# First two products of a transformer kernel interleaved by depth block, their transfers in that order, and the last product finished bank by bank

## What is computed

```python
def _even_mixer(x, norm_g, w_in, ...):
    h = _rmsnorm(x, norm_g)
    qa, ka, va, qb, kb, vb = _split(h @ w_in, EVEN_SPLITS)   # 512, 128, 128, 512, 512, 512 columns
    qa = _rmsnorm(qa per head, qn_a)
    ...
def rmsnorm(x, g):
    y = xf * lax.rsqrt(jnp.mean(xf * xf, axis=-1, keepdims=True) + RMS_EPS)
    return (y * g).astype(x.dtype)
# last: x = x + merged @ w_out; out = rmsnorm(x, g_final)
```

## Time and profile before

| | |
|---|---|
| median of the runs | 973.5 us |
| the profiled execution | 973.11 us |
| its span | 971.3 us |
| PE, share of the span | 99% |
| VectorE | 73% |
| ACT | 57% |
| POOL | 16% |

### The profile page before, as it was taken

One profiled execution on the slowest core, in us unless ns is written; L12 is line 12 of the kernel. 1 busy time (PEld: TensorE's weight loads), 2 busy tenths in 40 slices (PEclk: granted clock), 3 DMA queues, 4 the chain that ended last, 5 costly groups with the idle time before them and its releaser, 6 DMA issues.

```text
span 971.3 us, 13894 instructions
## 1 busy us (share of the span) xinstructions
PE 963.1 (99%) x5288; PEld 825.0 (85%) x5288; DVE 705.0 (73%) x1093; ACT 555.1 (57%) x957; POOL 154.9 (16%) x189
## 2 busy tenths in 40 slices
PE   9999999999999999999999999999999999999997
PEld 8878888888888888888888888888888888988885
DVE  6888676776666767786667656666758989888884
ACT  6688665444555553455456444554535857866662
POOL 2741018920001102220001000000550110000000
PEclk9999999999999999999999999999999999999999
DMA  9885535565554664445555665555544453543631
GB/s 338 302 226 190 181 130 181 188 229 183 173 194 155 216 215 131 131 135 212 174 174 181 203 211 185 173 186 183 206 153 152 154 194 111 173 153 129 217 131 44
DMA packets 110338, 174.72 MB, mean 180 GB/s; under 512 B 4288, under 2 KB 73024, under 8 KB 110272
## 3 DMA queue, kind: packets, MB, share of 16 engines
q1 hardware_dynamic: 109840, 173.40, 53.3%
q10 hardware_dynamic: 432, 0.44, 0.1%
HBM read 172.78 MB, written 1.05 MB: 179 GB/s over the span
## 4 chain that ended last, share of the span: by engine, by line
PE 92%; DVE 3%; POOL 1%; issue 1%; DMA 1%; SPq 1%; ACT 0%; POOLq 0%; DVEq 0%
PE ps L572 24%; PE ps L542 14%; PE ps L500 9%; PE ps L445 8%; PE ps L447 8%; PE ps L446 8%; PE ps L546 7%; PE ps L509 5%; PE ps L521 2%; PE ps L700 1%; PE ps L680 1%; PE ps L530 1%; PE ps L668 1%; DMA xs<-in_x 1%; PE ps L624 1%
## 5 line engine op out<-in xcount | busy, mean ns | idle before, releaser
L1557 DVE TENSOR_TENSOR wlo<-raw,whi 128x1024 fp32r<-128x1024 f32 x312 | 373.9, 1237 | 13.7 <-PE ps L572 8.3
L1047 ACT ACTIVATE whi<-raw 128x1024 fp32r<-128x1024 f32 x312 | 315.8, 1049 | 35.0 <-PE ps L572 22.0
L572 PE MATMUL ps<-whi,ur 128*128 128x512 f32 x656 | 182.0, 390 | 0.0
L572 PEld LDWEIGHTS ps<-whi,ur 128*128 128x128 f32 x656 | 121.1, 188 | 23.5
L542 PE MATMUL ps<-hT,whi 128*128 128x512 f32 x592 | 140.5, 389 | 0.0
L542 PEld LDWEIGHTS ps<-hT,whi 128*128 128x128 f32 x592 | 110.7, 188 | 22.8
L445 PE MATMUL ps<-whi,hT 128*128 128x512 f32 (+1 forms) x312 | 122.1, 391 | 0.0
L447 PE MATMUL ps<-whi,hT 128*128 128x512 f32 (+1 forms) x312 | 120.0, 385 | 0.0
L446 PE MATMUL ps<-wlo,hT 128*128 128x512 f32 (+1 forms) x312 | 119.9, 384 | 0.0
L1924 DVE TENSOR_TENSOR arena<-ps,arena 128x256 f32<-128x256 f32 x80 | 33.4, 423 | 98.6 <-ACT arena L1289 98.6
L1289 ACT ACTIVATE arena<-ps 128x256 f32<-128x256 f32 x80 | 30.2, 385 | 127.2 <-PE ps L546 127.2
(11 more groups left out here) (232 smaller groups left out, 1284.4 us busy)
## 6 DMA issues: line engine op xcount, KB each, us to landing
raw<-in_w SPq DMA_DIRECT2D x64, 1024.0 KB, 5.6
raw<-in_w_in SPq DMA_DIRECT2D x34, 1024.0 KB, 4.9
raw<-in_w_in_o SPq DMA_DIRECT2D x24, 1024.0 KB, 5.2
raw<-in_w_out_o SPq DMA_DIRECT2D x8, 1024.0 KB, 4.8
raw<-in_w_in_e SPq DMA_DIRECT2D x5, 1024.0 KB, 13.2
raw<-in_w_mem SPq DMA_DIRECT2D x4, 1024.0 KB, 11.1
raw<-in_w_out_e SPq DMA_DIRECT2D x4, 1024.0 KB, 4.9
raw<-in_w_out SPq DMA_DIRECT2D x4, 1024.0 KB, 4.8
```

The source lines that it names most:

```text
L572: mm = e.matmul(bank("acc", stage, 2 * tb + i), x[p], t[p % 2][:, 0, 512 * i:512 * i + 512], start=start and p == 0, stop=stop and p == 2)
L1047: e.activation(split_half(i)[0], raw_half(i), ACT.Copy).then_inc(*up("hi", ("hi", i)))
L1557: e.tensor_tensor(l, raw_half(i), h.bitcast(F32), ALU.subtract).then_inc(*up("lo", ("lo", i)))
```

## The change

The first two products, qa and ka, take turns: two depth blocks of qa, then the same two depth blocks of ka (for both position blocks), four times. Within qa a pass now runs over both position blocks before the next pass. The transfers come in that order: x block 0 first, on SP's queue, then the weights, with the ka tile in four transfers of 256 KB and the x blocks 0 to 3 one by one. ACT and VectorE make the parts in that order; the high part of x block 0 is VectorE's. There are eight warm-up products for ten. What ACT and VectorE do behind these first weights keeps its order. At the end the last four depth blocks run bank by bank, the final norm is made for each bank, and the last scale is split at column 640 for 512 between VectorE and ACT.

```diff
@@ sp_program
+                first_block(0)
+                piece(0, 0, 1, "w0")
+                piece(0, 1, 1, "w1")
+                first_block(1)
+                piece(2, 0, 2, "w6")
+                piece(0, 2, 1, "w2")
+                first_block(2)
+                piece(0, 3, 1, "w3")
+                first_block(3)
+                piece(2, 2, 2, "w8")
+                piece(1, 0, 1, "w4")
+                first_pair(2)
+                piece(1, 1, 1, "w5")
+                piece(2, 4, 2, "w9")
+                first_pair(3)
+                piece(1, 2, 2, "raw1")
+                piece(2, 6, 2, "raw2")
...
-            for tb, i in ((0, 1), (0, 0), (1, 0)):
+            for tb, i in ((0, 0), (0, 1), (1, 0)):
+                n = (slice(0, 640), slice(640, 1024))[i]
...
@@ pe_program
+            def first_products():
+                qa, ka = ([take("mm", label, tb) for tb in range(2)] for label in ("qa", "ka"))
+                for j in range(4):
+                    i = first_half["qa"] + j
...
+                    for k in (2 * j, 2 * j + 1):
...
+                        for tb in range(2):
+                            e.matmul(qa[tb], xh[tb], h[:, k % 2, :], start=k == 0, stop=False)
+                        w.wait_ge(*at("lo" if k % 2 else "lo0", i))
+                        for tb in range(2):
+                            e.matmul(qa[tb], xh[tb], l[:, k % 2, :], start=False, stop=False)
+                        w.wait_ge(*at("xl", "E", k))
+                        for tb in range(2):
+                            mm = e.matmul(qa[tb], xl[tb], h[:, k % 2, :], start=False, stop=k == 7)
...
+                    i = first_half["ka"] + j // 2
...
+                    for tb in range(2):
+                        for k in (2 * j, 2 * j + 1):
...
+                            mm = mm3(ka[tb][:, 0:256], x, (h[:, k % 4, :], l[:, k % 4, :]), k == 0, k == 7)
...
-            for i in range(10):
+            for i in range(8):
                 e.matmul(psum[7][:, 0:128], arena[:, 0:128], arena[:, 128:256], start=True, stop=True)
-            qa_product()
-            for j in range(2):
-                n_half("ka", j, 256, "E")
...
+            first_products()
...
             for tb in range(2):
-                for d in range(4):
-                    acc_part("sec", ur[0], d, t[d], tb, by_bank if d == 3 else by_pass, False, d == 3)
+                for c in range(2):
+                    for d in range(4):
+                        acc_part("sec", ur[0], d, t[d], tb, [(p, c) for p in range(3)], False, d == 3)
@@ act_program
+            def weights_first():
+                for j in range(4):
+                    for k in range(2):
+                        w.wait_ge(*((S[f"w{2 * j + k}"], 16) if j < 3 else loaded(1)))
+                        e.activation(split_half(j)[0][:, k, :], raw_half(j)[:, k, :], ACT.Copy).then_inc(
+                            *up("hi", ("hi", j) if k else ("hi0", j)))
+                        if j or k:
+                            x_first(2 * j + k)
+                    i, t = 4 + j // 2, slice(2 * (j % 2), 2 * (j % 2) + 2)
...
+                    e.activation(split_half(i)[0][:, t, :], raw_half(i)[:, t, :], ACT.Copy).then_inc(
...
-            e.dma_start(xT0[:, 0, :], A["xT"][0:128, :]).then_inc(S["t0"], 16)
-            weights_to(6)
+            weights_first()
             row_squares("E", x3, osb, [(S["x0"], 16), (S["x1"], 16)])
             hn_squares("qa")
             used("qa", 3)
...
@@ dve_program
-            weights_to(6)
+            e.tensor_scalar(hT[0][:, 0, :], xT0[:, 0, :], gain[:, G_ATT:G_ATT + 1], None, ALU.mult).then_inc(*up("dev", ("xh", "E", 0)))
+            weights_first()
             row_reciprocals("E")
             hn_sums("qa")
...
                 for i in range(2):
+                    n = slice(512 * i, 512 * i + 512)
+                    acc_added("sec", banks=(2 * tb + i,))
                     w.wait_ge(*at("x", "sec", 2 * tb + i))
...
+                    e.tensor_tensor(fin[:, tb, n], x3[:, tb, n], rows[:, R_FIN + 512 * i:R_FIN + 512 * i + 512], ALU.mult).then_inc(
+                        *up("dst", ("xg", tb, i)))
+                    w.wait_ge(*at("sq", "fin", tb, i))
...
-                e.scalar_tensor_tensor(fin[:, tb, 0:512], x3[:, tb, 0:512], s1, rows[:, R_FIN:R_FIN + 512],
-                                       ALU.mult, ALU.mult).then_inc(*up("dst", ("fin", tb, 0)))
+                e.tensor_scalar(fin[:, tb, 0:640], fin[:, tb, 0:640], s1, None, ALU.mult).then_inc(*up("dst", ("fin", tb, 0)))
```

More of the change, by code:

```diff
@@ L35 @@
 SEMS = ["mm", "wd", "tp", "qk", "pv", "hi", "xh", "aev", "ex", "asq", "lo", "xl", "dev", "dst", "sc", "po",
-        "w0", "w1", "w2", "w3", "w4", "w5", "w6", "w7", "raw0", "raw1", "raw2", "raw3", "x0", "x1", "t0", "t1", "t2", "t3", "t4", "id", "c", "c2", "g", "b", "m", "out"]
+        "w0", "w1", "w2", "w3", "w4", "w5", "w6", "w7", "w8", "w9", "raw0", "raw1", "raw2", "raw3", "x0", "x1", "t0", "t1", "t2", "t3", "t4", "t5", "id", "c", "c2", "g", "b", "m", "out"]
 PAIRS = [(0, 2), (1, 3), (4, 6), (5, 7)]
@@ L377, in sp_program @@
                 if m == 0:
[L378 to L392, removed]
+                    first_weights()
+                elif m < 3:
+                    pass
                 elif m == 3:
@@ L1034, in weights_to @@
                 for i in range(done[0], min(n, NH)):
[L1035 to L1041, removed]
                     if tiles[i // 2][0] == "memT":
                         continue
-                    w.wait_ge(*((S[f"w{i // 2 + 4}"], 16) if i in (4, 6) else loaded(i // 2)))
+                    w.wait_ge(*((S["w7"], 16) if i == 6 else loaded(i // 2)))
                     if i >= NHI:
@@ L1048, in weights_to @@
                 done[0] = max(done[0], n)
+            def weights_first():
[7 more added lines that the diff above has]
+                    i, t = 4 + j // 2, slice(2 * (j % 2), 2 * (j % 2) + 2)
+                    w.wait_ge(*((S[("w6", "w8", "w9")[j]], 16) if j < 3 else loaded(2)))
+                    e.activation(split_half(i)[0][:, t, :], raw_half(i)[:, t, :], ACT.Copy).then_inc(
+                        *up("hi", ("hi", i) if j % 2 else ("hi0", i)))
+                done[0] = 6
             def used(label, j):
@@ L1544, in weights_to @@
                     h, l = split_half(i)
[L1545 to L1551, removed]
                     if tiles[i // 2][0] == "memT":
@@ L1558, in weights_to, with weights_first @@
                 done[0] = max(done[0], n)
+            def weights_first():
+                for j in range(4):
+                    h, l = split_half(j)
+                    for k in range(2):
+                        w.wait_ge(*(at("hi", j) if k else at("hi0", j)))
+                        e.tensor_tensor(l[:, k, :], raw_half(j)[:, k, :], h[:, k, :].bitcast(F32), ALU.subtract).then_inc(
+                            *up("lo", ("lo", j) if k else ("lo0", j)))
+                        x_first(2 * j + k)
+                    i, t = 4 + j // 2, slice(2 * (j % 2), 2 * (j % 2) + 2)
+                    h, l = split_half(i)
+                    w.wait_ge(*(at("hi", i) if j % 2 else at("hi0", i)))
+                    if i >= NLO:
+                        w.wait_ge(*at("wd", i - NLO))
+                    e.tensor_tensor(l[:, t, :], raw_half(i)[:, t, :], h[:, t, :].bitcast(F32), ALU.subtract).then_inc(
+                        *up("lo", ("lo", i) if j % 2 else ("lo0", i)))
+                done[0] = 6
             def memory_low(blocks):
```

69 lines of the change are left out of this document (37 added, 32 removed).

## The result

The changed kernel takes 975.09 us (median of 15 runs, 974.46 to 976.47) beside 973.05 for the kernel before (15 runs). That is 2.0 us more by the medians; the ratio of the runs is 1.0025, 95% interval 1.0018 to 1.0032. The forecast was 974.7 in 973.2 to 976.0, so the time lies in the range and on the side that was named. Between "within", which had 0.83, and "slower", which had 0.15, it lies on the edge: the text's bound in us, 975.45, is not reached, while its 0.2% is just passed, by a ratio whose interval holds 1.002. The profiled execution is one of the lower group, 974.83 us with a span of 973.0.

A forecast was written before the change was run, and what follows sets the result against it. TensorE, busy 99% of the span, was taken to bound the kernel, so any new hole is paid in full. Lateness before qb of +1.4 and tail of -0.2 gave +1.2 on 973.5: 974.7 us, range 973.2 to 976.0.

The forecast's parts named there:

- within: Whole kernel: a time within about 0.2%, 1.95 us, of no change; chance 0.83.
- slower: Whole kernel: a time above 975.45 us; chance 0.15.
- The mechanism: Before qb: qa ends later, ACT's fixed order holds half 6 behind qa's squares, PE stands for about 1.85 us.
- rival 4: Front: small transfers land late, ACT waits for raw1 past 15.4; 975.7 or 976.3 for landings at 16.4 or 17; chance 0.15.
- The lateness: Start of qb: 1.5 us late by the sum, 24.05 for 22.56; taken as 1.4, span 1.2 to 2.0.
- The term for the first pair: First qa and ka blocks on PE: holes of 0.3 and 0.1 us waiting for low parts, 0.4 in all.
- It passed in full: From qb to the end: VectorE's chain is fed by PE, so the 0.9 us wait at kb's transposes swallows nothing; +1.4.
- Rival 2: At kb's transposes, 64.5 us: VectorE's chain less late than PE, so 0.9 us is swallowed; 973.8; chance 0.13.
- Rival 1: Front: PE's start 0.65 us earlier carries through to qb, not slower; 972.7; chance 0.10.
- Rival 3: POOL's first scale of qa's sums shut out by VectorE's low parts, 1.5 us later; 974.9; chance 0.07.
- The clock: TensorE in the new hole before qb: no fall of the granted clock expected, as it was still full in 967 to 968.
- The tail: After the last product: 0.1 each from the moved small step and the shorter last scale, 0.2 us saved (0 to 0.3).

The follow-up runs named there:

- lower group: Nine of the changed kernel's 15 runs, at 974.5 to 975.2 us.
- half6_first: Changed kernel with half 6 split before qa's squares on ACT and before their sums on VectorE; 972.88 us, ratio 0.9996 to the kernel before.
- pe_late: Kernel before with four 128x128 products added on PE between ka and qb, nothing moved on ACT or VectorE; 973.96 us, ratio 1.0006.
- hole_filled: Changed kernel with eight 128x128 products put between the first products and qb, ACT's order untouched; 974.89 us, ratio 1.0017 to the kernel before.
- changed_again: The changed kernel run again unaltered, for another profile; 975.24 us, ratio 1.0024 to the kernel before; its profiled execution took 976.72.
- upper group: Six of the changed kernel's 15 runs, at 976.1 to 976.5 us.
- head_only: The change without its tail part: last product, final norm and output transfers as in the kernel before; 976.42 us, ratio 1.0027 to the kernel before.
- tail_only: Kernel before with only the change's tail part: last product and final norm by bank, last scale split at 640; 973.37 us, ratio 1.0000.

## Why the prediction was right, and where it was not

**The mechanism held.** The fixed order on ACT and VectorE, with half 6 behind the squares of a qa that now ends later, was named as the cost, and half6_first shows it: moving half 6 up on both takes back the whole 2 us. The steps behind qa's end were right: high part 0.97 after the squares, low part 1.09 after that, PE 1.34 (load) after that, 3.40 together for the 3.39 of the sum. The row squares were no limit, raw1 was taken at 14.68 (14.6 in the text), so rival 4 did not occur.

**The lateness was mis-sized: 1.99 for 1.4.** The term for the first pair failed: 0.4 of holes on a start at 5.0. Measured, the start is 4.73 and the loss 1.15, so the first pair ends 0.48 later than reckoned (8.64 for 5.0 + 2.76 + 0.4 = 8.16), and the squares start at 21.15 for 20.7. The step that was wrong is the price of a product there: 0.230 was taken from the run that starts at 5.67 and used for products ahead of it. A row at hand hinted at it, the warm-up's 4.53 us for 20 passes, beside 0.119 a pass for the twice as wide products of ka; but those are another kind of product (plain float32, two records for each), and only the inserts of pe_late and hole_filled showed them at half pace. Then, the sum said 1.5 and the text took 1.4; the shading had no row and went the wrong way. The text's span of 1.2 to 2.0 does not follow from its terms either: a start of 4.8 to 5.3 and holes of 0.4 to 0.8 give 1.3 to 2.2.

**It passed in full,** as forecast, and for the reason given: pe_late shows VectorE's chain to be as late as PE, with the wait at kb unchanged. Rival 2 is out. Rival 1 is out too, and for more than the reason given: even with the squares out of the way the early start carried nothing through to qb.

**Rival 3 did not occur.** POOL's first scale came at 22.56 and took 0.27 us, ahead of VectorE's low part at 23.21, in the order the text expected. A later step did meet VectorE:

```profile
24.69 1.07 POOL L2339 TENSOR_SCALAR stat<-stat 128x8 f32<-128x8 f32 x1
25.85 0.27 POOL L2335 TENSOR_SCALAR stat<-stat 128x8 f32<-128x8 f32 x1
```

It took 1.07 while the second low part ran until 25.57. The rule of the Trainium skill, page "SBUF — State Buffer", section "Who interferes with whom", agrees with that row. It does not show in the row between: POOL's instruction from 22.92 to 24.59, which also reads SBUF, overlaps the low parts from 23.21 on, and it took 1.67, as it did at 23.72 before with VectorE idle, while the two low parts took 2.36 for 2.35. For the long scale VectorE waited 0.23 us; its scaling of qa starts at 25.80, still no later than before (25.86). No run prices those 0.23.

**The clock was dismissed, wrongly.** The text expected no fall in the hole, because the clock was still 1.00 in 967 to 968, three us after the last product. The window right behind that one, in the trace of before, reads:

```profile
968.00:969.00 1.00, 0.00 (x0) 0.00 (x0) 0.01 (x1) 0.00 (x0) 0.00 (x0) 0.51 0.12 45
```

One row more would have shown the fall. And the inference was too strong: a stretch after which nothing ran shows when the clock fell there once, not that a shorter pause leaves it alone. In changed_again it fell after the work had been taken up again. Counting the times of the upper group as such falls, although only one of them was profiled, there was one in 6 of 15 executions, in 4 of 10, and in 4 of 7 of head_only; each costs some 1.3 to 1.6 us. It is not in the medians of the lower group, and it widens the upper side: with it the runs reach 976.5, past the range's 976.0.

**The tail** was put at -0.2 and showed 0.13 in the changed kernel's trace; alone it showed no gain. Behind the add the 0.2 is there (3.00 for 3.20). The step that was missed is that VectorE now waits idle for the last bank: 0.50 from the product's start to the add, 0.85 in tail_only, where it was 0.43.

**Why the total still came close: luck.** The forecast started from 973.5, the median of three runs; over 15 runs before is 973.05. The lateness was 0.6 larger than taken, and the base 0.45 smaller. Two errors of opposite sign leave 974.7 beside a lower group whose median is 974.93. For the chance of "slower" the same two do not cancel: the measured 1.99 - 0.13 is close under a bound of 1.95, with the runs at the lower clock on top, so 0.15 looks too little.

The best kernel of the study is half6_first, 972.88 and 972.84 in two sets of runs, which cannot be told from the kernel before.

## What to carry to other kernels

When a product is made to end later, look on every other engine for the instruction in program order behind the one that consumes it: what stands there waits too, whether it needs the product or not, and here moving that one step up, on both engines that make it, took back the whole loss. A gain at the start of a kernel should be priced with the pace of the products that run there, not with that of the steady stream. A hole of 2 us in TensorE's stream can cost more later, here another 1.3 to 1.6 us in some executions; when a trace is quoted for the clock, read on to the row where it falls.

## What was not expected of the hardware

The first products step by 0.42 instead of 0.23 until 5.65 to 7 us (and the small ones by 0.227 instead of 0.12), while the granted clock of these windows reads 1.00. After a pause of 1.8 us the granted clock fell from 1.00 to 0.5 more than a microsecond after TensorE had resumed, and by the times this happens in only some of the executions; with the same delay filled by eight small products none of 11 did. An add on VectorE that waited idle for a product began 0.49 to 0.50 us after the start of that product in seven profiles and 0.85 in that of tail_only.
